# A router in strips, modulation ahead of the expert splits, and products of constants in TensorE's waits

## What is computed

```python
for l in range(DEPTH):                                   # DEPTH = 2
    hl = modulate(rms_norm(xl, norm1_g[l]), ml[:, :, 0], ml[:, :, 1])
    out_l, out_c = token_mixers(hl, hc, w_in[l], ...)    # attention, pooling, Hyena, merge
    xl = xl + ml[:, :, 2] * out_l
    hl2 = modulate(rms_norm(xl, norm2_g[l]), ml[:, :, 3], ml[:, :, 4])
    # context tokens likewise in layer 0
    f = grouped_moe(tokens, w_router, router_bias, w_gate_e[l], w_up_e[l], w_down_e[l])
    xl = xl + ml[:, :, 5] * f

def grouped_moe(h, ...):
    aff = sigmoid(h @ w_router)                          # (tokens, 16): the router's logits
    # best group of 4 experts, two experts of it, shares wsel
    for e in range(16):
        out += gates[:, e:e+1] * ((silu(h @ w_gate[e]) * (h @ w_up[e])) @ w_down[e])
```

## Time and profile before

| | us |
|---|---|
| median of 3 runs | 1628.83 |
| lowest and highest | 1625.04, 1630.57 |
| profiled execution | 1625.21 |
| its span, first to last instruction | 1623.5 |
| PE busy | 1459.7 (90%) |
| DVE busy | 880.4 (54%) |
| ACT busy | 633.9 (39%) |
| POOL busy | 364.8 (22%) |
| granted clock of TensorE, mean | 0.961 |

### The profile page before, as it was taken

The page is one execution under the profiler, slowest core; times in us unless marked ns, Lnnn a source line. Parts: engine busy times, 40 slices in busy tenths (PEclk is TensorE's granted clock), DMA queues, the critical chain, the costliest instruction groups (busy, mean ns, idle before and its releaser), DMA issues. The chain is left out here.

```text
span 1623.5 us, 19902 instructions
## 1 busy us (share of the span) xinstructions
PE 1459.7 (90%) x7944; PEld 1067.5 (66%) x7944; DVE 880.4 (54%) x1258; ACT 633.9 (39%) x853; POOL 364.8 (22%) x196
## 2 busy tenths in 40 slices
PE   6898999979999996799999987798988997998887
PEld 1565778756777763678888873596868995333334
DVE  4721577686222335888999965756593555111112
ACT  2422221266322224377777754442255443010102
POOL 0322332310322220211010003292323661000000
PEclk9999999989999998899999998899999998999998
DMA  9447231202556661699999984062303667899994
GB/s 347 165 184 272 88 104 53 79 20 70 191 185 204 205 243 54 263 353 400 411 405 406 399 294 143 26 198 87 106 20 131 242 231 271 342 422 419 422 421 173
DMA packets 118157, 367.31 MB, mean 226 GB/s; under 512 B 7918, under 2 KB 73776, under 8 KB 87216
## 3 DMA queue, kind: packets, MB, share of 16 engines
q1 hardware_dynamic: 109296, 334.62, 54.9%
q0 software_dynamic: 8768, 31.40, 5.2%
HBM read 353.40 MB, written 12.58 MB: 225 GB/s over the span
## 5 line engine op out<-in xcount | busy, mean ns | idle before, releaser
L803 POOL TENSOR_TENSOR w_lo<-ring,w_hi 128x1024 fp32r<-128x1024 f32 x120 | 297.5, 2490 | 606.4 <-ACT w_hi L1754 606.4
L950 PE MATMUL bank<-h_hi,w_hi 128*128 128x512 f32 (+1 forms) x768 | 275.1, 358 | 15.8 <-DVE h_lo L2131 10.4
L951 PE MATMUL bank<-h_hi,w_lo 128*128 128x512 f32 (+1 forms) x768 | 264.6, 345 | 0.0
L952 PE MATMUL bank<-h_lo,w_hi 128*128 128x512 f32 (+1 forms) x768 | 264.6, 345 | 0.0
L950 PEld LDWEIGHTS bank<-h_hi,w_hi 128*128 128x128 f32 x768 | 148.0, 193 | 56.8 <-issue 25.2
L952 PEld LDWEIGHTS bank<-h_lo,w_hi 128*128 128x128 f32 x768 | 148.2, 193 | 16.9
L951 PEld LDWEIGHTS bank<-h_hi,w_lo 128*128 128x128 f32 x768 | 148.4, 193 | 16.5 <-issue 1.4
L1754 ACT ACTIVATE w_hi<-ring 128x1024 fp32r<-128x1024 f32 x120 | 125.5, 1053 | 72.2 <-DMA ring<-in_w_in 35.2
L950 PE MATMUL bank<-w_hi,h_hi 128*128 128x512 f32 (+1 forms) x384 | 141.2, 368 | 10.2 <-DVE w_lo L2485 5.1
L952 PE MATMUL bank<-w_lo,h_hi 128*128 128x512 f32 (+1 forms) x384 | 137.6, 358 | 0.0
L951 PE MATMUL bank<-w_hi,h_lo 128*128 128x512 f32 (+1 forms) x384 | 137.4, 358 | 0.0
(11 more groups left out here) (343 smaller groups left out, 2793.1 us busy)
## 6 DMA issues: line engine op xcount, KB each, us to landing
ring<-in_w_in SPq DMA_DIRECT2D x52, 1024.0 KB, 5.1
ring<-in_w_down_e SPq DMA_DIRECT2D x36, 1024.0 KB, 7.3
ring<-in_w_up_e SPq DMA_DIRECT2D x34, 1024.0 KB, 7.5
mix<-in_w_gate_e SPq DMA_DIRECT2D x32, 1024.0 KB, 7.9
operands_plain<-in_w_gate_e SPq DMA_DIRECT2D x29, 1024.0 KB, 22.6
ring<-in_w_mod SPq DMA_DIRECT2D x24, 1024.0 KB, 7.0
mix<-in_w_mod SPq DMA_DIRECT2D x24, 1024.0 KB, 5.0
mix<-in_w_up_e SPq DMA_DIRECT2D x22, 1024.0 KB, 23.5
```

What stands on the lines that cost most here:

```text
L803: pool.tensor_tensor(w_lo[:, slot], rview(raw, 8)[:, :, x * P:(x + 1) * P], w_hi[:, slot].bitcast(F32), ALU.subtract).then_inc(w_l, 1)
L950: first = mm(dst, stat[0], mov[0], start=start, stop=False)
L951: mm(dst, stat[1], mov[0], start=False, stop=False)
L952: return first, mm(dst, stat[0], mov[1], start=False, stop=stop)
```

## The change

1. On ACT the splits of the first three chunks go from ahead of the modulation to behind the token rows; on DVE its first split goes to behind the one-hots.
2. The router's weights are padded to 32 columns, and each tile's product is done as one product for each 128 tokens, into strips of 32 partitions of the bank. The logits then need one copy and one transposition, and the exponential reads 16 of every 32 columns.
3. DVE adds the squares of a tile ahead of its wait for the next output tile, where they were added behind it.
4. At seven places in PE's program stand products of constants, `keep_busy(bank, n)`: 128x512, plain float32, into a bank that nobody reads.

```diff
-        wrt = area(6144, DK * E_N).rearrange("p (k e) -> p k e", k=DK)
+        wrt = area(6144, DK * 32).rearrange("p (k e) -> p k e", k=DK)
-        logit = area(6528, 512)[0:E_N, :]
+        logit = area(6528, 128)
+            constants = square[:].rearrange("p i t -> p (i t)")
+
+            def keep_busy(b, n):
+                for _ in range(n):
+                    mm(bank[b][:, :], ones, constants, start=True, stop=True)
...
                     pe.wait_ge(z_x[l - 1], 16 * l)
                     filters(l, 1)
+                    keep_busy(6, 5)
...
                 scores(0)
                 scores(1)
+                keep_busy(4, 3)
...
+                keep_busy(4, 2 - l)
                 norm_sum_added(2 * l + 1, T)
+                keep_busy(4, 4 - 2 * l)
...
-                    last = mm(bank[7][0:E_N, 0:T], wrt[:, k, :], hTs[2 * l + 1][:, k, 0:T], start=k == 0, stop=k == DK - 1)
+                    for j in range(nt):
+                        last = mm(bank[7][32 * j:32 * j + 32, 0:P], wrt[:, k, :], hTs[2 * l + 1][:, k, j * P:(j + 1) * P],
+                                  start=k == 0, stop=k == DK - 1)
                 last.then_inc(q_lg[l], 1)
                 pe.wait_ge(q_ex[l], 2 * l + 1)
-                for j in range(nt):
-                    last = tp(bank[6][:, j * E_N:(j + 1) * E_N], logit[:, j * P:(j + 1) * P], ident[0:E_N, 0:E_N])
-                last.then_inc(q_lg[l], 1)
+                tp(bank[6][:, 0:32 * nt], logit[0:32 * nt, :], ident[0:32 * nt, 0:32 * nt]).then_inc(q_lg[l], 1)
...
                     filters(l + 1, 0)
+                    keep_busy(1, 4)
                     spectra_a(l + 1, 0)
                     spectra_b(l + 1, 0)
+                    keep_busy(1, 5)
...
                 A(small[:, 14:15], fin_g[:, 0:1], ACT.Exp)
-                splits(range(XH))
                 act.wait_ge(m_d[l], 2 * l + 2)
                 norm_act_scale(2 * l + 1, T, S)
...
-                A(logit[:, 0:T], bank[7][0:E_N, 0:T], ACT.Copy).then_inc(q_ex[l], 1)
+                A(logit[0:32 * nt, :], bank[7][0:32 * nt, 0:P], ACT.Copy).then_inc(q_ex[l], 1)
                 act.wait_ge(q_lg[l], 2 * l + 2)
-                A(rt[:, 1, 0:nt * E_N], bank[6][:, 0:nt * E_N], ACT.Exp, scale=-1.0).then_inc(q_ex[l], 1)
+                A(rt[:, 1, 0:nt * E_N].rearrange("p (j e) -> p j e", e=E_N),
+                  bank[6][:, 0:32 * nt].rearrange("p (j e) -> p j e", e=32)[:, :, 0:E_N], ACT.Exp, scale=-1.0
+                  ).then_inc(q_ex[l], 1)
...
+                splits(range(XH))
...
                 for m in range(DK):
+                    for k in [m - 2] * (m >= 3) + [m - 1] * (m == DK - 1):
+                        squares_added(k)
                     dve.wait_ge(o_pe[l], DK * l + m + 1)
...
-                    if m >= 3:
-                        squares_added(m - 2)
                 dve.wait_ge(o_d[l], 16 * l + 8 * S)
-                for k in range(DK - 2, DK):
-                    squares_added(k)
+                squares_added(DK - 1)
                 norm_dve(2 * l + 1, T)
...
-                splits(range(1))
-
...
+                splits(range(1))
                 rows_in(0)
```

More of the change, by code:

```diff
@@ L2889 @@
     data["fin_g"] = cols(final_g)
-    data["w_router"] = np.asarray(w_router).reshape(DK, P, E_N).transpose(1, 0, 2)
+    data["w_router"] = np.pad(np.asarray(w_router).reshape(DK, P, E_N).transpose(1, 0, 2), ((0, 0), (0, 0), (0, 32 - E_N)))
     data["router_bias"] = np.broadcast_to(np.asarray(router_bias), (P, E_N))
```

## The result

The changed kernel takes 1620.1 us (median of 17 runs, 1616.66 to 1624.81), the kernel before 1629.69 (17 runs, 1624.62 to 1635.03). The ratio of the runs is 0.9946, interval 0.9936 to 0.9956: 8.8 us less of 1630 (the two medians lie 9.6 apart). One later execution of the changed kernel took 2439.86 us at a granted clock of 0.556; it is left out. The forecast was 1614.0, range 1607.5 to 1620: the sign is right, the gain is too large, and the time lies just outside the range. So the two traces differ by only 0.9 us in all, and are to be read place by place.

The account below looks back on a forecast made before the run. Layer 0's experts were taken as bound by TensorE, layer 1's by loads, so only their start could move. Terms -7.7 - 1.7 + 0.4 - 0.8 - 2.9 = -12.7 gave 1612.5 or 1616.1 us; 1614.0 was taken, range 1607.5 to 1620.

Parts of the forecast that it names:

- What bounds the kernel, and that a shift passes through: Layer 0's experts bound by TensorE, layer 1's by loads; earlier logits move everything behind them as one.
- Layer 0's router, -7.7: Routing in layer 0 starts at 638.78 for 646.48 through squares, moved splits and strips: -7.7 us (-6.9 to -8.3).
- The chain of 1.1: Layer 0's router, from PE's last product to DVE's routing: 1.1 us (bounds 0.8 and 1.39) for 1.39.
- The squares, 0.77 and 0.50: Earlier adds of squares take 0.77 us off the start of layer 0's norm; one 0.50 add goes ahead in layer 1.
- Moved splits at nothing: Layer 0's moved splits cost nothing, covered by ACT's wait of 12.16 us and DVE's of 5.00 before the experts.
- Layer 1's router, -2.9: PE is slower than ACT in layer 1's router; strips bring logits at 1358.96 for 1361.86: -2.9 us (-2.3 to -3.2).
- The products, -1.7, +0.4 and -0.8: Products of constants: -1.7 us at layer 0's attention, +0.4 at layer 1's, -0.8 at the end of layer 0.
- the two bases: Whole kernel: 1612.5 us against the profiled execution, 1616.1 against the median; 1614.0 was taken between them.
- clock won nowhere: Rival: work behind the products stays at half clock, layer 1's attention loses 3.1 us; -7.5, 1617.7 us; chance 0.12.
- half of the gain stays in the experts' start: Rival: half of layer 0's router gain of 7.7 us is lost where the experts start; -8.9, 1616.3 us; chance 0.07.
- Clock held everywhere: Rival: full clock at layer 0's attention (-3.0 us) and the end of layer 0 (-2.5); -16.1, 1609.1 us; chance 0.10.
- strips in line: Rival: router strips do not run side by side, 0.31 us a record; +7.5, 1632.7 us; chance 0.03.

Follow-up runs that it names:

- late_logits_0: The changed kernel with twelve products of constants ahead of the last tile's strips in layer 0, making the logits late; ratio 0.9999 to the kernel before.
- changed_again: The changed kernel itself, unaltered, measured again on the same chip as three other kernels; ratio 0.9943 to the kernel before.
- order_strips: The kernel before with the moved splits and the strips alone, without the squares and without products of constants; ratio 0.9948 to the kernel before.

## Why the prediction was wrong, point by point

- **What bounds the kernel, and that a shift passes through: right for layer 1, and for layer 0's experts once they run** (the 199.3 us). At their start a part may be lost: late_logits_0 got 8.6 us for 12.3. The missing part need not belong to that start: in its trace the first experts take 79.5 us for 82.0 and 80.2 in the changed kernel's two, the stretch behind layer 1's routing 253.4 for 255.9 twice, and both vary between traces. By 0.7 the 7.4 us of layer 0's router would be worth 5.2, with 2.5 of layer 1 an estimate of 7.7; the runs without products gave 8.5 to 11.1.
- **Layer 0's router, -7.7: nearly right.** -6.5 at routing and -0.86 before it for the squares make -7.4. The modulation follows DVE as forecast. The strips end 0.9 us behind DVE's last tile (638.74 for 637.83) where I took 0.56. ACT's last modulation ends with that tile (637.23 + 0.60), so it is not the reason: PE begins the seventh tile's strips only at 637.66, takes the eighth's right behind them, and needs 1.08 us for the two, at half clock (granted 0.50 from 637.66 to 638.74). The chain of 1.1 measured 1.15 (638.74 to 639.89).
- **The squares, 0.77 and 0.50: right in size, not sure to come.** At equal clock they give 0.86 and, in layer 1, 0.47. But where the norm's sum runs at half clock, 0.94 is lost again: the norm takes about 3.14 or 4.07 with the new order, 4.00 or 4.94 with the old (4.38 and 4.57 in one trace each).
- **Moved splits at nothing: right** (ACT's wait of 7.52, DVE's of 3.72).
- **Layer 1's router, -2.9: the size nearly right (-2.5), the reason wrong.** I read PE's 5.98 us as the work of eight products, and took PE for the slower engine. It was half clock: at full clock the same product takes 3.95 and keeps pace with ACT. So I gave to the strips a gain that a held clock gives as well. The strips end 0.70 us behind ACT's last modulation (1357.95 for 1357.25), not 0.28. The product ahead of the sum I credited with 0, and of the two behind it the sum did not speak.
- **The products, -1.7, +0.4 and -0.8: here the sum failed.** They were to give 2.1 us and give nothing that can be measured (four kernels at 0.9939 to 0.9947). *Attention of layer 0*: its start is 2.3 us quicker in all nine traces with these products, but also in two of the eleven without them, and 0.9 quicker in a third; behind it some is given back, up to 1.1 us at the output projection and 0.9 at the norm's sum. So half clock there was a cost of most executions without products, and not of all, and the sum took what was gained there as gained at the end. *Attention of layer 1*: the +0.4 came to 0.1 in the changed kernel's two traces and to nothing in the other seven with these products. *End of layer 0*: the price of half clock stood in the row, but the products did not hold the clock over the transpositions, which wait for the gathered rows all the same. They take 5.99 to 6.23 us in the traces of before, and 5.38 to 6.48 in the seven with these products, under 5.9 only in changed_again.
- **Between the two bases I took 1614.0: wrong.** 17 runs of before give 1629.69, so that the profiled 1625.21 was a quick execution, as was the start of its trace. From 1629.69 the sum of -12.7 would have been 1617.0, inside 3.1 us of the result. So of the 6.1 us between forecast and result 3.0 are the base, 2.1 the products, and 1.0 is left.
- **Rivals.** They were priced from 1625.2. By the number "clock won nowhere", 1617.7, came nearest, but its reason did not: its +3.1 in layer 1 is 0.1, and attention of layer 0 did become quicker. From the median of before, "half of the gain stays in the experts' start", 1616.3, would be 1620.8. The first experts take 82.0 and 80.2 us in the changed kernel's traces, for 78.4, but 77.3 in order_strips, which has the same router: no fixed loss. "Clock held everywhere" fell at the end of layer 0, "strips in line" with 0.063 us a record.

What stays open: place by place the rows give 2.3 + 0.86 + 6.5 + 0.47 + 2.0 = 12.1 us, the runs 8.8. The two traces of the changed kernel are longer at two other places: the first experts (82.0 and 80.2 us, for 78.3 to 78.4 in three traces of before) and the stretch behind layer 1's routing (255.9 twice, for 252.0 to 255.8). At the first the granted clock is lower (0.86 and 0.88 for 0.91). Together they could take the missing 3.3 us and more, but they vary between traces of one kernel, and so few traces cannot say whether the change made them longer.

## What to carry to other kernels

Before a row's time is priced as work, look at the granted clock of its stretch: a product at half clock is shortened by less work and by a kept clock alike, and the two gains are not to be added. A gain read from one trace at half clock should be checked in a second trace of the same kernel, since the stretch may lie elsewhere there. Take the forecast's base from the median of the runs, not from the profiled execution; and to learn what a shift is worth, make it larger (12 products, 11 us) instead of trying to measure 2 us.

## What was not expected of the hardware

The stretches at half clock lie elsewhere in each execution. In most traces the same instructions take one of two times: attention's start 21.4 or 23.6 us, the first expert 17.1 or 18.7, the norm's sum 1.1 or 2.1. Half clock that is avoided at one place can turn up at the next: quick attention went with a slow norm sum in five traces of five without products between. One product of constants ahead of a product did not change its clock (6.12 us), three, the last two right behind the norm's sum, did (3.95).
